# Three chained blocks on one core: a PSUM bank by name for one transpose, rows spread by loads from DRAM instead of matmuls, and residual rows loaded stage by stage

## The reference, cut to what matters

```python
# block 1: y = mix(...) @ w_out;             x = x + rmsnorm(y) * norm_post
# block 2: y = mix(...) @ w_out_2;           x = rmsnorm(x + y) * final_g_2
# block 3:
mod = silu(c) @ w_ada + b_ada
shift, scale, gate = split(mod, 3)
h = rmsnorm(x, ln_g) * (1 + scale) + shift
p = h @ w_in + b_in            # also the mLSTM's input and forget gate logits, one column per head
#   mLSTM, 4 heads: the score of query t and key s is weighted by
#   exp(-M[t] + a[s]) inside a chunk, and by exp(prev - M[t]) * decay ... across chunks
y = concat(mlstm, nsa) @ w_out
x = rmsnorm(x + gate * y) * final_g
```

## Time and profile before

| | |
|---|---|
| runs | 2820.95, 2821.03, 2824.04 us; median 2821.03 |
| profiled execution, its own time | 2821.26 us |
| its span | 2819.5 us |
| mean granted TensorE clock | 0.997 |
| busy in the span | PE 2788.5, PEld 2313.4, DVE 1416.3, ACT 1073.6, POOL 365.5 us |

### The profile page before, as it was taken

How to read it: one execution, slowest core, us unless ns; L and a number is a source line. 1 busy time by engine, 2 the same in 40 slices (tenths; PEclk the granted TensorE clock), 3 DMA queues, 4 the chain that set the end, 5 groups by cost and what they waited for, 6 DMA issues and landing times.

```text
span 2819.5 us, 37532 instructions
## 1 busy us (share of the span) xinstructions
PE 2788.5 (99%) x15080; PEld 2313.4 (82%) x15080; DVE 1416.3 (50%) x2521; ACT 1073.6 (38%) x1818; POOL 365.5 (13%) x627
## 2 busy tenths in 40 slices
PE   8999999999999999999999999999999999999998
PEld 7888877888889878888888888887777777788888
DVE  6686644436337363655654335335544553545534
ACT  5333234454226343322222335434443544333322
POOL 6456254100001000000100001000000000000011
PEclk9999999999999999999999999999999999999999
DMA  7566465324325454566665334542222223223433
GB/s 202 146 187 122 126 145 124 105 83 161 109 93 183 139 165 135 174 185 187 201 187 173 103 97 129 121 97 68 71 68 71 68 68 97 76 82 83 150 97 120
DMA packets 445054, 352.47 MB, mean 125 GB/s; under 512 B 73869, under 2 KB 396269, under 8 KB 440657
## 3 DMA queue, kind: packets, MB, share of 16 engines
q1 hardware_dynamic: 408722, 241.93, 30.6%
q0 software_dynamic: 36160, 108.14, 13.0%
HBM read 322.81 MB, written 22.81 MB: 123 GB/s over the span
## 4 chain that ended last, share of the span: by engine, by line
PE 96%; DVE 1%; DMA 1%; ACT 1%; issue 0%; POOL 0%; SPq 0%; DVEq 0%; ACTq 0%
PE bank L3628 59%; PE bank L3664 16%; PE bank L3634 4%; PE bank L3687 2%; PE bank L3586 2%; PE bank L2389 1%; PE bank L2440 1%; PE bank L2416 1%; PE bank L667 1%; PE bank L2510 1%; PE bank L2462 1%; PE bank L730 1%; DMA ring<-in_w_in 1%; PE bank L3561 1%; PE bank L694 0%; PE bank L663 0%
## 5 line engine op out<-in xcount | busy, mean ns | idle before, releaser
L3777 DVE TENSOR_TENSOR ring_parts<-ring,ring_hi 128x1024 fp32r<-128x1024 f32 x420 | 510.6, 1228 | 744.8 <-ACT ring_hi L3736 740.6
L3736 ACT ACTIVATE ring_hi<-ring 128x1024 fp32r<-128x1024 f32 (+1 forms) x424 | 441.3, 1051 | 602.7 <-DMA ring<-in_w_in 302.7
L3628 PE MATMUL bank<-A_parts,ring_hi 128*128 128x512 f32 x1552 | 619.0, 399 | 1.1 <-DVE ring_parts L3777 1.1
L3628 PE MATMUL bank<-A_parts,ring_parts 128*128 128x512 f32 x1552 | 606.3, 391 | 0.0
L3628 PE MATMUL bank<-X_parts,ring_hi 128*128 128x512 f32 x1360 | 529.6, 389 | 0.0
L3628 PE MATMUL bank<-B_parts,ring_hi 128*128 128x512 f32 x1224 | 479.6, 392 | 0.0
L3628 PEld LDWEIGHTS bank<-A_parts,ring_hi 128*128 128x128 f32 x1552 | 292.1, 188 | 65.6 <-issue 7.6
L3628 PEld LDWEIGHTS bank<-A_parts,ring_parts 128*128 128x128 f32 x1552 | 291.8, 188 | 62.8
L3628 PEld LDWEIGHTS bank<-X_parts,ring_hi 128*128 128x128 f32 x1360 | 255.6, 188 | 50.9
L3628 PE MATMUL bank<-B_parts,ring_parts 128*128 128x512 f32 x752 | 292.7, 389 | 0.0
L3628 PEld LDWEIGHTS bank<-B_parts,ring_hi 128*128 128x128 f32 x1224 | 230.6, 188 | 51.9 <-issue 5.9
(11 more groups left out here) (574 smaller groups left out, 3853.5 us busy)
## 6 DMA issues: line engine op xcount, KB each, us to landing
ring<-in_w_in SPq DMA_DIRECT2D x288, 512.0 KB, 3.8
ring<-in_w_out SPq DMA_DIRECT2D x96, 512.0 KB, 3.7
work<-in_w_ada POOLq DMA_DIRECT2D x96, 512.0 KB, 5.0
ring<-in_w_in SPq DMA_DIRECT2D x48, 256.0 KB, 3.7
ring<-in_w_mem_kv SPq DMA_DIRECT2D x16, 512.0 KB, 4.1
x_keep<-X POOLq DMA_DIRECT2D x8, 1024.0 KB, 4.6
X<-x_keep POOLq DMA_DIRECT2D x8, 1024.0 KB, 10.2
X<-in_x SPq DMA_DIRECT2D x4, 1024.0 KB, 9.8
```

Source lines behind the costliest of these rows:

```text
L3628: mm = nc.tensor.matmul(K.ps(st)[0:w + (t["beside"] or 0), 0:t["n"]], lhsT=wp[:, j, :], rhs=columns(ap, kk), start=first, stop=end)
L3736: nc.scalar.activation(slot_view[key](ring_hi), slot_view[key](ring), ACT.Copy).then_inc(s_hi, 1)
L3777: nc.vector.tensor_tensor(lo, slot_view[key](ring), slot_view[key](ring_hi), ALU.subtract).then_inc(s_lo, 1)
```

## The change

Four edits.

- The turn of the gate rows takes bank 7 by name; `mg_rows` takes 4 and 5 and `cmp` 6 and 7 by name, as they had from the rotation.
- The head rows: GpSimd's queue stores the two sets of 4 rows to DRAM once, and for each head loads the two rows spread over 128 partitions, into `E` and a new buffer `query_w` (256 KB each), in `pool_ml_qk`. The two matmuls, their banks and the copy of rows to partition 32 go.
- The modulation gate: after the last `ada_sum` its 2048 numbers are stored to DRAM, and each projection stage of block 3 loads its 512 columns spread over 128 partitions. `wo_gate` goes on TensorE and ScalarE.
- `pool_wo` in all three blocks loads, per stage, what that stage needs: blocks 2 and 3 the stage's columns of the 4 row tiles (4 loads of 256 KB) and of the gain (256 KB), block 1 one row tile (1 MB) and the gain's columns. From stage 1 on, the loads wait for the previous stage's loads and for its first bank to be full.

```diff
     def pool_wo(pool, st):          # block 1
-        if st[2] == 0:
+        n = st[2]
+        cols = slice(n * NC, (n + 1) * NC)
+        if n == 0:
             pool.wait_ge(K.y_done, K.y_base[1] + KT)
-            for tt in range(TT):
-                pool.dma_start(X[:, tt, :], T["x"][0, tt * P:(tt + 1) * P, :]).then_inc(s_back, 16)
-            pool.dma_start(gain_post, T["norm_post"][0].partition_broadcast(P)).then_inc(s_fg, 16)
+        else:
+            pool.wait_ge(s_fg, 16 * n)
+            pool.wait_ge(*bk.filled(("wo", 1, n - 1), 0))
+        pool.dma_start(gain_post[:, cols], T["norm_post"][0][cols].partition_broadcast(P)).then_inc(s_fg, 16)
+        pool.dma_start(X[:, n, :], T["x"][0, n * P:(n + 1) * P, :]).then_inc(s_back, 16)
...
     def vec_wo_row(vec, L, st, tt): # block 2; blocks 1 and 3 likewise
-        if st[0:3] == ("wo", 2, 0) and tt == 0:
-            vec.wait_ge(s_back, 16 * TT)
-            vec.wait_ge(s_fg, 16)
+        if st[0] == "wo" and tt == 0:
+            vec.wait_ge(s_back, 16 * TT * (st[2] + 1))
+            vec.wait_ge(s_fg, 16 * (st[2] + 1))
...
+    def pool_sum(pool, st):
+        if st[1] < ADA_PARTS - 1:
+            return
+        pool.wait_ge(s_mod, 1)
+        with nc.allow_non_contiguous_dma(reason="small per-channel parameters"):
+            pool.dma_start(gate_d.rearrange("(k p) -> p k", p=P), mod[:, 2 * KT:3 * KT]).then_inc(s_gate_st, 16)
...
-    K.wo_mids[3, 0] = {0: [num[3]], 2: [tr[3], ("mix_parts", 3, 3)], 4: [("wo_gate", 3, n) for n in range(4)]}
+    K.wo_mids[3, 0] = {0: [num[3]], 2: [tr[3], ("mix_parts", 3, 3)]}
...
         if kind == "mg_rows":
-            K.uses[st] = [("i", "S", 1), ("f", "S", 2)]
+            K.uses[st] = [("i", 4, 1), ("f", 5, 2)]
...
         elif kind == "cmp":
-            K.uses[st] = [(0, "S", 1), (1, "S", 1)]
+            K.uses[st] = [(0, 6, 1), (1, 7, 1)]
...
         elif kind == "turn":
-            K.uses[st] = [(0, 7 if st in in_pairs else "S", 1)]
+            K.uses[st] = [(0, 7 if st in in_pairs or st == ("turn", "gates", 0) else "S", 1)]
...
         elif kind == "ml_s":
-            K.uses[st] = [(key, "S", 1) for key in ("m", "w", ("o", 0), ("o", 1), "s")]
+            K.uses[st] = [(key, "S", 1) for key in (("o", 0), ("o", 1), "s")]
...
     def pool_mg_exp(pool, st):
         pool.wait_ge(s_gate, 5)
-        pool.dma_start(negM[32:32 + M_H, :], wst[0:M_H, :]).then_inc(s_below, 16)
+        pool.dma_start(rows_d[0], negM[0:M_H, :]).then_inc(s_rows_st, 16)
+        pool.dma_start(rows_d[1], wst[0:M_H, :]).then_inc(s_rows_st, 16)
+
+    def pool_ml_qk(pool, st):
+        h = st[1]
+        if h == 0:
+            pool.wait_ge(s_rows_st, 32)
+            pool.wait_ge(s_nsa, len(pairs) // TT)
+        else:
+            pool.wait_ge(*bk.released(("ml_s", h - 1), "s"))
+        pool.wait_ge(*bk.filled(st, ("k", 1)))
+        for dst, r in ((E, 0), (query_w, 1)):
+            pool.dma_start(dst, rows_d[r, h].partition_broadcast(P)).then_inc(s_rows, 16)
...
     def pool_wo(pool, st):          # block 3, and block 2 without the gate
...
+            pool.wait_ge(s_gate_row, 16 * st[2])
+            pool.wait_ge(s_back, 16 * TT * st[2])
+            pool.wait_ge(s_fg, 16 * st[2])
+            pool.wait_ge(*bk.filled(("wo", 3, st[2] - 1), 0))
+        pool.dma_start(gate_sb[:, at], K.gate_d[at].partition_broadcast(P)).then_inc(s_gate_row, 16)
+        for tt in range(TT):
+            pool.dma_start(X[:, tt, at], x_keep[tt * P:(tt + 1) * P, at]).then_inc(s_back, 16)
+        pool.dma_start(K.work[:, 2 * D + at.start:2 * D + at.stop], T["final_g_3"][at].partition_broadcast(P)).then_inc(s_fg, 16)
...
     def pe_ml_s(pe, st):
         h = st[1]
-        if h == 0:
-            pe.wait_ge(s_below, 16)
-        bk.take(pe, st, "m")
-        bk.take(pe, st, "w")
-        for key, r in (("m", 0), ("w", 32)):
-            nc.tensor.matmul(ps(st, key), lhsT=K.ident[r:r + M_H, r + h:r + h + 1].to_broadcast([M_H, P]), rhs=negM[r:r + M_H, :], start=True,
-                             stop=True).then_inc(bk.full_sem(st, key), 1)
...
     def vec_ml_s(vec, L, st):
-        vec.wait_ge(*bk.filled(st, "m"))
+        vec.wait_ge(s_rows, 32 * (h + 1))
```

More of the change, by code:

```diff
@@ L1559, in pool_wo @@
     def pool_wo(pool, st):
-        if st[2] == 0:
+        n = st[2]
+        cols = slice(n * NC, (n + 1) * NC)
+        if n == 0:
             pool.wait_ge(K.y_done, K.y_base[2] + KT)
-            for tt in range(TT):
-                pool.dma_start(X[:, tt, :], x_keep[tt * P:(tt + 1) * P, :]).then_inc(s_back, 16)
-            pool.dma_start(fg, T["final_g_2"].partition_broadcast(P)).then_inc(s_fg, 16)
+        else:
+            pool.wait_ge(s_back, 16 * TT * n)
+            pool.wait_ge(s_fg, 16 * n)
+            pool.wait_ge(*bk.filled(("wo", 2, n - 1), 0))
+        for tt in range(TT):
+            pool.dma_start(X[:, tt, cols], x_keep[tt * P:(tt + 1) * P, cols]).then_inc(s_back, 16)
+        pool.dma_start(fg[:, cols], T["final_g_2"][cols].partition_broadcast(P)).then_inc(s_fg, 16)
     def pe_gate(pe, st):
@@ L1944, in vec_sum @@
         L.settle()
+        if part == ADA_PARTS - 1:
+            vec.sem_inc(s_mod, 1)
     for st in ada_stages():
@@ L1949, in modulation @@
     K.c_params = pool_params
-    K.stage("pool", ada=pool_ada)
+    K.stage("pool", ada=pool_ada, ada_sum=pool_sum)
     K.stage("act", ada=act_ada)
@@ L2034, in block3 @@
     K.mix_early[3] = (8, K.work_parts[:, early_at:early_at + 6 * SEQ].rearrange("p (k t) -> p k t", t=SEQ))
-    assert early_at + 6 * SEQ <= lo_at
+    query_w = K.work[:, early_at + 6 * SEQ:early_at + 7 * SEQ]
+    assert early_at + 7 * SEQ <= lo_at
     assert max(a.at[0], a2.at[0], s.at[0]) <= lo_at
@@ L2982, in vec_ml_t @@
             vec.wait_ge(K.y_done, K.y_base[3] + 8 + i + 1)
-    def pe_wo_gate(pe, st):
-        n = st[2]
-        bk.take(pe, st, "g")
-        for j in range(4):
-            c = 2 * KT + 4 * n + j
-            mm = nc.tensor.matmul(ps(st, "g")[:, j * P:(j + 1) * P], lhsT=K.mod[:, c:c + 1].to_broadcast([P, P]),
-                                  rhs=K.ident[:, :], start=True, stop=True)
-        mm.then_inc(bk.full_sem(st, "g"), 1)
-    gate_sb = K.work[:, 3 * D:4 * D]
-    s_gsb = K.sem("gate_row_ready")
-    def act_wo_gate(act, L, st):
-        n = st[2]
-        act.wait_ge(*bk.filled(st, "g"))
-        if n == 0:
-            act.wait_ge(K.y_done, K.y_base[3] + KT)
-        nc.scalar.activation(gate_sb[:, n * NC:(n + 1) * NC], ps(st, "g"), ACT.Copy).then_inc(bk.free_sem(st, "g"), 1)
+    gate_sb = K.work[:, 3 * D:4 * D]
     def vec_wo_row(vec, L, st, tt):
@@ L3006, in vec_wo_row @@
         w = c.stop - c.start
-        if st[0:3] == ("wo", 3, 0) and tt == 0:
-            vec.wait_ge(s_back, 16 * TT)
-        vec.wait_ge(*bk.released(("wo_gate", 3, min(st[2], 3) if st[0] == "wo" else 3), "g"))
+        if st[0] == "wo" and tt == 0:
+            vec.wait_ge(s_gate_row, 16 * (st[2] + 1))
+            vec.wait_ge(s_back, 16 * TT * (st[2] + 1))
         vec.wait_ge(*bk.filled(st, tt))
@@ L3033, in act_final @@
         nc.scalar.activation(X[:, tt, 0:LEFT], X[:, tt, 0:LEFT], ACT.Copy, scale=K.rstd_out[:, tt:tt + 1]).then_inc(K.s_left, 1)
-    for n in range(4):
-        K.uses[("wo_gate", 3, n)] = [("g", 4 + n, 1)]
     script.insert(script.index(("norm", 3, TT - 1)) + 1, ("b3_tables", 0))
@@ L3071, in block3 @@
         [(slice(6, 7), gated(6).unsqueeze(1)), (slice(7, 8), yT[:, 7:8, :])] if g == 3 else [(slice(2 * g, 2 * g + 2), yT[:, 2 * g:2 * g + 2, :])]
-    K.stage("pool", norm3=pool_norm, mg_exp=pool_mg_exp, tile3=pool_tile, mz_back=pool_mz_back, b3_tables=pool_tables, wo3=pool_wo)
+    K.stage("pool", norm3=pool_norm, ml_qk=pool_ml_qk, mg_exp=pool_mg_exp, tile3=pool_tile, mz_back=pool_mz_back, b3_tables=pool_tables, wo3=pool_wo)
     K.stage("pe", turn=pe_turn, mg_rows=pe_mg_rows, mg_nat=pe_mg_nat, cmp=pe_cmp, cmp_end=pe_cmp_end, cmp2=pe_cmp2, nsa_s=pe_nsa_s, nsa_t=pe_nsa_t,
-            nsa_v=pe_nsa_v, nsa_cs=pe_nsa_cs, nsa_ct=pe_nsa_ct, ml_qk=pe_ml_qk, ml_s=pe_ml_s, ml_n=pe_ml_n, ml_t=pe_ml_t,
-            wo_gate=pe_wo_gate)
+            nsa_v=pe_nsa_v, nsa_cs=pe_nsa_cs, nsa_ct=pe_nsa_ct, ml_qk=pe_ml_qk, ml_s=pe_ml_s, ml_n=pe_ml_n, ml_t=pe_ml_t)
     K.stage("act", final3=act_final, tile3=act_tile, turn=act_turn, mg_rows=act_mg_rows, mg_exp=act_mg_exp, cmp_end=act_cmp_end, cmp2=act_cmp2, nsa_s=act_nsa_s, nsa_t=act_nsa_t, nsa_cs=act_nsa_cs, nsa_ct=act_nsa_ct,
-            xc_parts=act_xc_parts, ml_qk=act_ml_qk, ml_s=act_ml_s, ml_n=act_ml_n, wo_gate=act_wo_gate)
+            xc_parts=act_xc_parts, ml_qk=act_ml_qk, ml_s=act_ml_s, ml_n=act_ml_n)
     def vec_xc_parts(vec, L, st):
```

30 lines of the change are left out of this document (16 added, 14 removed).

## The result

| | before | after |
|---|---|---|
| median, us | 2820.99 (2820.62 to 2824.04, 4 runs) | 2805.99 (2805.47 to 2807.25, 4 runs) |
| profiled execution, own time / span | 2821.26 / 2819.5 | 2807.25 / 2805.4 |
| mean granted TensorE clock | 0.997 | 0.998 |

What follows compares the result with a forecast made beforehand. TensorE bounds the kernel, busy for 2788.5 of 2819.5 us. The terms 6.4 + 4.2 + 3.6 = 14.2 us take 2821.26 to 2807.0, the median 0.2 lower: 2806.8 us, own range 2805 to 2809.

Steps and rivals of the forecast that it cites:

- the turn's bank: Turn of the gate rows: naming its bank ends the wait for L2564; 3.10 idle + 1.24 + 2.08 lower clock = 6.4 us.
- head rows: Score products of four heads: removing the two spreading matmuls saves 4 x 1.06 = 4.2 us of TensorE's line.
- modulation gate: Block 3's projection: without the spreading matmuls of `wo_gate` TensorE saves 3.49 + 0.08 = 3.6 us.
- residual rows by stage: Projections of all blocks: smaller loads per stage count 0; bounds 0.5 us gained or lost at each block's first stage.
- rival (a): At the turn, the clock falls anyway near 1750 and only the idle goes: 10.9 us less, 2810.1 us; chance 0.14.
- The cover: Head rows' loads, from the keys' end to L2510: over 21 us; loads would have to take 16 us to cost anything.
- two tiles: Work of TensorE between the keys' end and L2510, with the score products: over 21 us, VectorE needing some 5.
- the lead: Weight ring at block 3's projection: removing `wo_gate` would cut its lead from 6.1 to 2.5 us; the smaller burst restores it.
- the slot that lands late: Ring slot in block 3's projection, read at 2664.25 after 10.16 us of waiting; TensorE needs it only at 2672.7.
- rival c: Projection stages: 12 load bursts collide with the weight ring, at 4 us each 48 us slower, 2855 us; chance 0.05.

## Why the prediction was right, and where it was off

| term | predicted | measured |
|---|---|---|
| the turn's bank | 6.4 | 6.53 (3.26 idle, 3.27 clock); 6.8 to 6.9 against four other executions |
| head rows | 4.2 | 5.05 |
| modulation gate | 3.6 | 2.96 alone, 3.62 with staging |
| residual rows by stage | 0 | 0.0 alone, 0.7 beside the gate |
| sum | 14.2 | 15.2 by the trace, 15.0 by the medians |

**The turn's bank** was right in mechanism and size. The point was to see that L2564 does not write the turn's data. The turn part is the same to 0.01 us with the bank names alone and with the whole change. That the size came out to a tenth was luck: the idle time before the turn was 3.10 us in the trace that the prediction read and up to 3.98 in others. The rule behind rival (a), from the Trainium skill ("TensorE: Matmul & The Clock Gate", "What's actually happening"), would have let some executions keep the fall. In the eight profiled executions in which the bank is named, the turn's records take 1.89 us each time, the length at full clock.

**The head rows** were mis-sized: 1.06 us per head was the time from the first spreading matmul to the first score product, and nothing was taken for the change of kind of matmul behind it, though the same prediction did count 0.08 for that at the gate. The score products are 0.20 us shorter without those matmuls ahead (why, no run separates): 4 x 1.26 = 5.04, and 5.05 was measured. The cover was judged by head 3, the tightest. The prediction's "two tiles" there are one tile and one slot of the projection, which is what gives its 21 us. For L2510 (now L2547) the cover holds, 11.2 us measured beyond the loads. It was followed to that product alone: the next group, L2520 (now L2557), runs out first.

**The modulation gate** was right at 3.6 only because staging was there. The prediction said so ("cuts the lead from 6.1 to 2.5 us; the smaller burst gives it back") but looked at the slot that lands late, which indeed never stops TensorE. What it missed is the order behind that slot: row tiles, their squares, then the split three slots on, where the lead ran out. Its 0 for staging is right for that edit alone and its 3.6 for the gate only with staging; taken one by one, 0.7 us change hands between the two. The store of the gate took 12.6 us for 8 KB, where 9.2 for a load was the nearest row, and a 256 KB load takes 4.4; with 1100 us until it is wanted it costs nothing. The Trainium skill's rule on transfers below 512 B ("DMA: Bandwidth & Descriptors", "Specifications") agrees in direction with these times; no run separates it from other causes.

**The bursts** (rival c) cost TensorE nothing: no wait of TensorE for the ring in any projection stage of the changed kernel, with 3.2 MB more through GpSimd's queue (111.30 against 108.14). The Trainium skill's advice to batch to 1 MiB ("DMA: Bandwidth & Descriptors", "Measured (HBM→SBUF, 128 partitions, SWDGE, issued from GpSimd)") would have spoken for the loads of before; here the smaller ones were worth 0.7 us in the late part, beside the gate.

The sum was 1.0 us short of the trace's 15.2, 0.85 of it from the head rows and 0.1 from the turn; the median lies in the forecast's own range of 2805 to 2809.

## What to carry to other kernels

Ask of each wait what its releaser frees, data or a bank: a wait for a bank from a rotation can be bought off with a name, if another bank stands free by then. Look at the granted clock behind an idle gap of TensorE before pricing it: here 3.3 us of idle cost 3.3 more at the lower clock, 4.2 us cost 2.7 more, and 1.9 us nothing. Price a removed matmul group with its neighbours, not by its own records. Follow the cover of a load to every group that hangs on the waiting engine, not only to the first one. When the lead of a weight ring shrinks, follow the delay through the in-order scripts of the engines that feed it, not only to the slot that lands late; and when gains are smaller than the scatter of the runs, compare starts of the same work within the trace, and check on kernels that should agree how well that measure repeats.

## What the runs showed that I had not expected

Staging makes one of VectorE's additions (L3031) much longer, once in each of three projection stages of block 3: 3.46, 3.40 and 3.68 us, and 2.87 to 2.92 with staging alone. VectorE's timeline of the changed kernel:

```profile
2664.63 0.69 DVE L3031 TENSOR_TENSOR X<-X,work 128x512 f32<-128x512 f32 x1
2665.24 0.68 DVE L3029 TENSOR_TENSOR work<-bank,work 128x512 f32<-128x512 f32 x1
2665.96 3.46 DVE L3031 TENSOR_TENSOR X<-X,work 128x512 f32<-128x512 f32 x1
```

and GpSimd's:

```profile
2665.66 0.54 POOL L2328 DMA_DIRECT2D work<-in_final_g  x1
2666.29 2.57 POOL L2335 TENSOR_TENSOR X<-X,work 128x512 f32<-128x512 f32 x2
```

The addition, with both inputs in SBUF, starts 0.33 us ahead of GpSimd's first multiplication, yet ends only after GpSimd's two multiplications (2668.86); L3029, with one input in a bank, keeps its 0.68. Before the change the longest such addition took 1.08 us. GpSimd's multiplications now stand behind the DMA issues of their stage and come as a pair while VectorE is at the row tiles. In the kernel without staging four multiplications in a row left the additions at 1.07; what makes the difference I have not separated. The Trainium skill ("SBUF — State Buffer", "Who interferes with whom") says that a VectorE instruction with two SBUF inputs contends with a GpSimd instruction that reads SBUF; the rows agree, 3.46 against 0.69 us. No wait of TensorE in that projection comes from it, but it takes 2.8 us of VectorE's slack at the very place where the ring's lead is shortest. A version that issues a stage's loads ahead of these multiplications was not tried.
